# Latent attention of a two-layer block: the 1/rms of the latents applied when queries, keys and values are evicted, and the rotary keys computed in the gate columns' job

## What is computed

```
def rms_norm(x, g):
    y = x * rsqrt(mean(x * x, axis=-1) + EPS)
    return y * g

q_lat, kv_lat, k_rope = split(z, (256, 128, 32))          # z = h @ w_in, per token
q  = (rms_norm(q_lat, g_q_lat) @ w_uq)                    # 4 heads x (64 + 32)
kv = (rms_norm(kv_lat, g_kv_lat) @ w_ukv)                 # 4 heads x (64 keys + 64 values)
q_rope = apply_rope(q[..., 64:96], rot)                   # grid tokens only
k_rope = apply_rope(k_rope, rot)                          # grid tokens only, one for all heads
k = concatenate([k_nope, broadcast(k_rope to 4 heads)])   # 64 + 32
y = softmax(q k^T * 96**-0.5) v
```

## Time and profile before

| what | us |
|---|---|
| median of 3 executions | 4300.83 |
| lowest and highest | 4300.26, 4307.57 |
| the profiled execution, its own time | 4302.52 |
| its span, first to last instruction | 4300.8 |
| layer 0, from the first latent product to the first turn of queries | 57.86 to 174.48 |
| layer 1, the same | 2406.18 to 2509.91 |

### The profile page before, as it was taken

The page is one execution under the profiler, slowest core; times in us unless marked ns, Lnnn a source line. Parts: engine busy times, 40 slices in busy tenths (PEclk is TensorE's granted clock), DMA queues, the critical chain, the costliest instruction groups (busy, mean ns, idle before and its releaser), DMA issues.

```text
span 4300.8 us, 62883 instructions
## 1 busy us (share of the span) xinstructions
PE 3689.4 (86%) x25844; PEld 2503.2 (58%) x25844; DVE 1177.2 (27%) x2860; ACT 769.2 (18%) x1604; POOL 127.7 (3%) x184
## 2 busy tenths in 40 slices
PE   7699999997999599999997669998978957777785
PEld 4355675665776377777775445666657734444443
DVE  0333342425642411111111152325246131111111
ACT  2221322012212200000001321312122120100101
POOL 0000000000000000000000000000000000000000
PEclk9799999998999699999999679898968979999998
DMA  4172111010011199999998101110100239999998
GB/s 185 69 275 97 42 45 44 11 69 1 25 69 69 67 341 343 328 346 351 344 342 321 44 0 37 50 49 30 69 1 30 103 108 383 378 379 381 382 373 304
DMA packets 326559, 740.25 MB, mean 172 GB/s; under 512 B 7808, under 2 KB 79488, under 8 KB 326288
## 3 DMA queue, kind: packets, MB, share of 16 engines
q1 hardware_dynamic: 314800, 695.29, 44.4%
q0 software_dynamic: 11616, 43.05, 3.5%
HBM read 713.09 MB, written 25.21 MB: 172 GB/s over the span
## 4 chain that ended last, share of the span: by engine, by line
PE 66%; DMA 16%; DVE 10%; ACT 5%; issue 3%; DVEq 0%; ACTq 0%; SPq 0%; POOL 0%; POOLq 0%
PE bank L544 11%; PE bank L962 9%; PE bank L472 7%; PE bank L935 7%; PE bank L465 5%; DMA ring<-in_w_e_up 5%; PE bank L926 4%; DMA ring<-in_w_e_gate 4%; PE bank L835 3%; DMA f_rows<-work,idx 3%; PE bank L634 3%; ACT work L1039 3%; DMA ring<-in_w_e_down 3%; PE bank L546 2%; DVE work L1487 2%
## 5 line engine op out<-in xcount | busy, mean ns | idle before, releaser
L544 PE MATMUL bank<-HT,ring 128*128 128x256 f32 x2560 | 637.9, 406 | 15.9 <-DVEq L1552 7.8
L544 PEld LDWEIGHTS bank<-HT,ring 128*128 128x128 f32 x2560 | 517.9, 205 | 122.6 <-issue 25.3
L962 PE MATMUL bank<-ring,work 128*96 128x512 f32 (+1 forms) x1408 | 472.7, 604 | 30.1 <-DMA ring<-in_w_e_down 28.2
L926 PE MATMUL bank<-ring,work 128*64 128x256 f32 x1536 | 384.1, 408 | 130.8 <-DMA ring<-in_w_e_up 71.9
L935 PEld LDWEIGHTS bank<-work,ring 128*64 128x64 f32 x11264 | 475.7, 139 | 16.8 <-issue 15.0
L935 PE MATMUL bank<-work,ring 128*64 128x96 f32 x11264 | 481.9, 249 | 4.2 <-DVEq L2023 3.0
L926 PEld LDWEIGHTS bank<-ring,work 128*64 128x64 f32 x1536 | 218.2, 147 | 271.1 <-DMA ring<-in_w_e_up 90.1
L927 PE MATMUL bank<-ring,work 128*64 128x256 f32 (+1 forms) x1536 | 369.2, 379 | 0.0
L962 PEld LDWEIGHTS bank<-ring,work 128*96 128x96 f32 (+1 forms) x1408 | 167.8, 152 | 298.7 <-issue 265.9
L1039 ACT ACTIVATE work<-bank,small 128x512 f32<-128x512 f32 (+3 forms) x248 | 144.6, 583 | 958.7 <-PE bank L962 500.5
L472 PE MATMUL bank<-ring,HT 128*128 128x512 f32 (+2 forms) x960 | 310.8, 488 | 0.5 <-DVEq L1552 0.5
(11 more groups left out here) (180 smaller groups left out, 3408.4 us busy)
## 6 DMA issues: line engine op xcount, KB each, us to landing
ring<-in_w_e_gate SPq DMA_DIRECT2D x64, 2048.0 KB, 10.4
ring<-in_w_e_up SPq DMA_DIRECT2D x64, 2048.0 KB, 13.5
ring<-in_w_e_down SPq DMA_DIRECT2D x64, 2048.0 KB, 9.6
ring<-in_w_ada SPq DMA_DIRECT2D x24, 2048.0 KB, 8.8
ring<-in_w_e_gate SPq DMA_DIRECT2D x32, 1536.0 KB
ring<-in_w_e_up SPq DMA_DIRECT2D x32, 1536.0 KB, 7.1
ring<-in_w_e_down SPq DMA_DIRECT2D x32, 1536.0 KB, 9.9
ring<-in_w_gate SPq DMA_DIRECT2D x16, 2048.0 KB, 8.6
```

Of the source, the lines that this page charges most:

```text
L544: pe.matmul(b[:, 0:256], w[:, k, d4 * P:(d4 + 1) * P], HT[:, k, off:off + 256], start=(k == 0), stop=(k == KD - 1))
L926: pe.matmul(b[0:64, 0:256], e_xs[:, k, 0:64], w[:, k, 0:256], start=(k == 0), stop=(k == KD - 1))
L962: ins = pe.matmul(banks[6 + half][lo:lo + cap, :], e_hidT[:, at, 0:cap], w[:, k, half * 512:half * 512 + 512], start=(f == 0), stop=(f == ...
```

## The change

- The three blocks of latents are evicted by ACT twice: once squared into `a_sq`, once times the gain `g` into `a_ql` or `a_kv`, without the 1/rms. DVE no longer squares or scales.
- The sums of squares are made with the squares stationary and one column of ones moving, so that each token's sum stands on its own partition, one column for each tile (`squares_of`). Those of the queries stand ahead of the gate columns' job, those of the kv latent behind it. ACT's root and DVE's reciprocal are now on at most 6 columns.
- The six `tm` jobs of the rotary keys are gone. The gate columns' job takes 72 columns instead of 40, with the rotary keys on partitions 0 to 31 of the bank; six transposes turn them to tokens on partitions.
- The queries move from ring "a" and ACT to ring "d" and DVE, which scales a tile by its 1/rms as it evicts it and rotates it at once. The grid's tiles come first.
- Keys and values are scaled by 1/rms as ACT evicts them; ACT waits for the reciprocal (`mla_n`) once, ahead of them.
- The four rotary key tiles are rotated together, in six instructions, and copied to the four heads in one.
- TensorE waits for `mla_kv` (ACT) and `mla_rope` (DVE) before it turns queries and keys.

```diff
-                for t in range(NT):
-                    tm(w, 384, 32, t)
+                def squares_of(rows, tiles):
+                    b = job("a")
+                    for t in tiles:
+                        for i in rows:
+                            ins = pe.matmul(b[:, t:t + 1], a_sq[:, i, t * P:(t + 1) * P], ones[:, 0:1],
+                                            start=(i == rows[0]), stop=(i == rows[-1]))
+                    ins.then_inc(sems["a_done"], 1)
+
+                pe.wait_ge(sems["mla_q"], c.nth("mla_q"))
+                squares_of((0, 1), QT)
                 for off, n in SEG:
-                    fm(w, 416, 40, off, n)
+                    fm(w, 384, 72, off, n)
                 used(n0)
-                pe.wait_ge(sems["mla_sq"], c.nth("mla_sq"))
...
-                pe.wait_ge(sems["mla_n"], c.nth("mla_n"))
+                pe.wait_ge(sems["mla_c"], c.nth("mla_c"))
+                squares_of((2,), range(NT))
                 uq = pk("w_uq").rearrange("p (i n) -> p i n", i=2)
-                for t in QT:
-                    b = job("a")
+
+                def queries(t):
+                    b = job("d")
                     for i in range(2):
                         ins = pe.matmul(b[:, 0:384], a_ql[:, i, t * P:(t + 1) * P], uq[:, i, :], start=(i == 0), stop=(i == 1))
-                    ins.then_inc(sems["a_done"], 1)
+                    ins.then_inc(sems["d_done"], 1)
+
+                first = [t for t in QT if t >= CT]
+                queries(first[0])
+                pe.wait_ge(sems["mla_kr"], c.nth("mla_kr"))
+                b = job("d")
+                for t in range(NT):
+                    ins = pe.transpose(b[:, t * 32:(t + 1) * 32], a_krf[0:32, t * P:(t + 1) * P], ident[0:32, 0:32])
+                ins.then_inc(sems["d_done"], 1)
+                for t in first[1:] + [t for t in QT if t < CT]:
+                    queries(t)
                 for t in range(NT):
                     b = job("a")
                     pe.matmul(b[:, :], a_kv[:, t * P:(t + 1) * P], pk("w_ukv"), start=True, stop=True).then_inc(sems["a_done"], 1)
+                pe.wait_ge(sems["mla_kv"], c.nth("mla_kv"))
                 pe.wait_ge(sems["mla_rope"], c.nth("mla_rope"))
```

ACT's part:

```diff
+                def latents(dst, sq, gain, off, n):
+                    act.wait_ge(sems["a_done"], c.nth("a_done"))
+                    b = bank()
+                    do(sq[:, off:off + n], b[:, 0:n], AF.Square)
+                    do(dst[:, off:off + n], b[:, 0:n], AF.Identity, scale=gain)
+                    act.sem_inc(sems["a_free"], 1)
+
+                def roots(i, tiles, width):
+                    act.wait_ge(sems["a_done"], c.nth("a_done"))
+                    b = bank()
+                    do(s_lat[:, i, tiles[0]:tiles[-1] + 1], b[:, tiles[0]:tiles[-1] + 1], AF.Sqrt, scale=1.0 / width, bias=cc("eps"))
+                    act.sem_inc(sems["a_free"], 1)
+                    act.sem_inc(sems["mla_r"], 1)
+
...
+                roots(0, QT, 256)
                 for off, n in SEG:
                     act.wait_ge(sems["a_done"], c.nth("a_done"))
                     b = bank()
-                    copy(a_kv[:, off:off + n], b[:, 0:n])
+                    copy(a_krf[0:32, off:off + n], b[0:32, 0:n])
+                    copy(gI[0:8, off:off + n], b[32:40, 0:n])
+                    copy(gF[0:8, off:off + n], b[64:72, 0:n])
                     act.sem_inc(sems["a_free"], 1)
...
+                act.sem_inc(sems["mla_kr"], 1)
+                roots(1, range(NT), 128)
+                act.wait_ge(sems["mla_n"], c.nth("mla_n"))
                 for t in range(NT):
                     act.wait_ge(sems["a_done"], c.nth("a_done"))
                     b = bank()[:, :].rearrange("p (h c) -> p h c", h=4)
-                    copy(a_ktm[:, t, :, 0:64], b[:, :, 0:64])
-                    copy(a_v[:, t, :, :], b[:, :, 64:128])
+                    do(a_ktm[:, t, :, 0:64], b[:, :, 0:64], AF.Copy, scale=s_lat[:, 1, t:t + 1])
+                    do(a_v[:, t, :, :], b[:, :, 64:128], AF.Copy, scale=s_lat[:, 1, t:t + 1])
```

DVE's part:

```diff
-                S(dve.reciprocal(a_r[:, 0, q0:T], a_r[:, 0, q0:T]))
-                S(dve.reciprocal(a_r[:, 1, :], a_r[:, 1, :]))
...
+                S(dve.reciprocal(s_lat[:, 0, QT[0]:NT], s_lat[:, 0, QT[0]:NT]))
+
+                def queries(t):
+                    dve.wait_ge(sems["d_done"], c.nth("d_done"))
+                    b = bank()
+                    ts(a_qtm[:, t, :, :], b[:, 0:384].rearrange("p (h c) -> p h c", h=4), s_lat[:, 0, t:t + 1], ALU.mult)
+                    dve.sem_inc(sems["d_free"], 1)
+                    if t >= CT:
+                        rope(a_qtm[:, t, :, 64:96], t, 4, a_tmp)
+
+                first = [t for t in QT if t >= CT]
+                dve.wait_ge(sems["mla_r"], c.nth("mla_r"))
+                S(dve.reciprocal(s_lat[:, 1, :], s_lat[:, 1, :]))
                 dve.sem_inc(sems["mla_n"], 1)
-                dve.wait_ge(sems["mla_tm"], c.nth("mla_tm"))
-                for t in range(CT, NT):
-                    rope(a_qtm[:, t, :, 64:96], t, 4, a_tmp)
-                    rope(a_kr[:, t, :], t, 1, a_tmp)
-                for t in range(NT):
-                    copy(a_ktm[:, t, :, 64:96], a_kr[:, t, :].unsqueeze(1).to_broadcast([P, 4, 32]))
+                queries(first[0])
+                dve.wait_ge(sems["d_done"], c.nth("d_done"))
+                b = bank()
+                copy(a_kr, b[:, 0:NT * 32].rearrange("p (t c) -> p t c", t=NT))
+                dve.sem_inc(sems["d_free"], 1)
+                rope(a_kr[:, CT:NT, :], None, NT - CT, a_tmp)
+                copy(a_ktm[:, :, :, 64:96], a_kr.unsqueeze(2).to_broadcast([P, NT, 4, 32]))
+                for t in first[1:] + [t for t in QT if t < CT]:
+                    queries(t)
                 dve.sem_inc(sems["mla_rope"], 1)
```

More of the change, by code:

```diff
@@ L413, in hybrid_layers @@
         s_soft = small[:, 412:424].rearrange("p (i t) -> p i t", i=2)
+        s_lat = small[:, 412:424].rearrange("p (i t) -> p i t", i=2)
         s_top = small[:, 424:488].rearrange("p (i c) -> p i c", i=8)
@@ L569, in mla @@
+                pe.wait_ge(sems["mla_q"], c.nth("mla_q"))
+                squares_of((0, 1), QT)
                 for off, n in SEG:
-                    fm(w, 416, 40, off, n)
+                    fm(w, 384, 72, off, n)
                 used(n0)
-                pe.wait_ge(sems["mla_sq"], c.nth("mla_sq"))
-                for off, n in QS:
-                    b = job("a")
-                    pe.matmul(b[:, 0:n], ones, a_sq[:, 0, off:off + n], start=True, stop=False)
-                    pe.matmul(b[:, 0:n], ones, a_sq[:, 1, off:off + n], start=False, stop=True).then_inc(sems["a_done"], 1)
@@ L577, in mla @@
-                for off, n in SEG:
-                    b = job("a")
-                    pe.matmul(b[:, 0:n], ones, a_sq[:, 2, off:off + n], start=True, stop=True).then_inc(sems["a_done"], 1)
-                pe.wait_ge(sems["mla_n"], c.nth("mla_n"))
+                pe.wait_ge(sems["mla_c"], c.nth("mla_c"))
+                squares_of((2,), range(NT))
                 uq = pk("w_uq").rearrange("p (i n) -> p i n", i=2)
-                for t in QT:
-                    b = job("a")
+                def queries(t):
+                    b = job("d")
@@ L1117, in mla @@
             def mla(L):
+                def latents(dst, sq, gain, off, n):
[10 more added lines that the diff above has]
+                    act.sem_inc(sems["mla_r"], 1)
                 for i in range(2):
                     for off, n in QS:
-                        act.wait_ge(sems["a_done"], c.nth("a_done"))
-                        b = bank()
-                        copy(a_ql[:, i, off:off + n], b[:, 0:n])
-                        act.sem_inc(sems["a_free"], 1)
+                        latents(a_ql[:, i, :], a_sq[:, i, :], pk("g_q")[:, i:i + 1], off, n)
+                act.sem_inc(sems["mla_q"], 1)
+                for off, n in SEG:
+                    latents(a_kv, a_sq[:, 2, :], pk("g_kv"), off, n)
+                act.sem_inc(sems["mla_c"], 1)
+                roots(0, QT, 256)
                 for off, n in SEG:
@@ L1572, in tab @@
                 def tab(name):
+                    if t is None:
+                        return cc(name).rearrange("p (t a f) -> p t a f", t=groups, a=2)
                     v = cc(name)[:, (t - CT) * 16:(t - CT + 1) * 16].rearrange("p (a f) -> p a f", a=2)
```

41 lines of the change are left out of this document (3 added, 38 removed).

## The result

| what | before, us | changed, us |
|---|---|---|
| median | 4304.14 (4 executions) | 4208.83 (4 executions) |
| lowest and highest | 4300.26, 4307.57 | 4205.88, 4213.57 |
| the profiled execution | 4302.52 | 4206.81 |
| its span | 4300.8 | 4205.1 |
| mean granted clock | 0.909 | 0.917 |

The ratio is 0.978, with a 95% interval of 0.9763 to 0.9797: 95 us faster. In two later comparisons, on two chips, the ratios were 0.9797 [0.9775, 0.982] and 0.9809 [0.9793, 0.9826]. So 84 to 95 us, by medians.

A forecast was written before the change was run, and what follows sets the result against it. The changed stage was taken as a serial chain, one engine after another. Gains 16.1 + 17.1 + 34.6 + 33.4 + 2 = 103.2 us took the profiled 4302.5 to 4199.3, the median to 4198 us, range 4186 to 4214.

The forecast's parts named there:

- its own unknowns: Whole kernel: narrow product price, spread copy, ACT's scale, warm start and small handovers give 4189 to 4207 us, chance 0.72.
- Ahead of G: Latent stage up to the gate job's end: narrow key jobs go, gate job quickens, sums added; gains 16.1 and 17.1 us.
- G: The moment the gate columns' job ends and the next weights are asked for: 119.85 us in layer 0, 2461.30 in layer 1.
- Behind G: Gate job's end to first turn of queries: 54.6 and 48.6 us become 20.0 and 15.2, gaining 34.6 and 33.4.
- The spread copy: DVE's one copy of 768 rotary key elements to the four heads, before the grid tiles, taken as 1.0 us.
- What starts behind: Turns and first scores: part of their half clock start may go, 1 us a layer, 2 us in all.
- Everything behind is shifted, not changed: Attention, other mixers and experts after the stage: keep their lengths, their weight requests shifting along; no gain or loss counted.
- fall in the new narrow work: Rival: clock falls in the sums and behind the gate job, costing 13 us, about 4211 us; chance 0.14.
- Late weights: Rival: first attention starts 35 us sooner after the request, one fetch about 8 us late, 4206 us; chance 0.05.
- 72 columns cost more than 40: Gate job: more stationary columns would cost more, one way of having no measurable gain; chance 0.01.
- The slower case: Rival: TensorE stays at half clock through the first attention, up to 150 us more, about 4347 us; chance 0.02.
- Its counterargument: Against half clock through the first attention: every row shows the clock returning within six us of work.

The follow-up runs named there:

- mixing them: Key and value jobs placed between the remaining query tiles on TensorE instead of behind them, against the changed kernel: median 4214.44 us.
- the comparison on one chip: Before and changed kernels, each plain and with layer 1's first attention 512 column score product made twice: means 4308.0 and 4221.2 us plain, 4301.5 and 4205.5 twice.
- the third trace of the changed kernel: The changed kernel run once more without any edit: median 4221.50 us, four executions.

## Why the prediction held, and which step was off

The forecast was 4198 us in a range of 4186 to 4214; the median was 4208.83. That lies in the range, but above the 4189 to 4207 that its own unknowns gave. Of the 11 us between, 3.3 are the base, since a fourth execution moved the median before from 4300.83 to 4304.14 us, and the rest is a gain that fell short: against the profiled execution the sum was 103.2 us and 95.7 were found. The mechanism of the stage was right; that the median fell inside the range has some luck in it, since the two later medians of the same kernel, 4214.38 and 4221.50 us, lie above it.

- *Ahead of G.* Expected 16.1 and 17.1 us, found 62.0 - 46.3 = 15.7 and 55.1 - 39.2 = 15.9 (from the first latent product to G). The narrow products cost 0.107 each (2.57 us for 24), just below the lower bound of 0.111. (Of my two rows for them, the products of 2 columns don't have the full stationary tile that I wrote: 64 partitions, not 128.) The gate job took 10.38 us against 10.3. What was short by a us was the latents themselves: 33.31 instead of 32.71 us in layer 0 and 27.11 instead of 25.83 in layer 1, since the clock rose one to three us later from its rest.
- *Behind G.* Expected 20.0 and 15.2 us to the first turn, found 19.9 and 14.8. The prices from the nearest rows held: an eviction with a scale 0.62 us plus its gap (0.65), a rotation 1.55 with gaps, ACT's twelve evictions 6.47 us (6.5). The spread copy was priced too dear, 1.0 us where it took 0.56, near its lower bound of 0.48. In layer 0 the bank of the third grid tile and the keys and values behind it ended the stage, as worked out; mixing them gained 3.7 us there, as expected, which the times of the whole didn't show.
- *What starts behind.* Two us expected, 0.6 + 0.8 found up to the first score. The transposes did run at 1.00 (124.10 to 134.40 us), so the rule in the Trainium skill, "TensorE: Matmul & The Clock Gate", Part 4: PE-mode transpose, that the full clock doesn't engage for them, isn't borne out here either.
- *"Everything behind is shifted, not changed".* This is the step that failed. It is right for the weights: TensorE waits for no transfer in layer 0's first attention, before or changed. It is wrong for the clock. I took the granted clock of an attention from 24 us of layer 0's, where it is 1.00, and let it stand for the whole of both. In the trace that I had, layer 0's has one fall in it, and layer 1's, which has no wide adaLN products between its own, works at a mean of 0.84, alternating. Such a stretch doesn't keep its length, not even from one execution of the same kernel to the next. In the first pair layer 1's attention took back 3.7 us and layer 0's 2.6; in the comparison on one chip, about nine us went with layer 1's.
- *The rivals.* The clock did not fall in the new narrow work in the trace of the result; in one of three traces of the changed kernel it did, in layer 0, and the gate job took 1.5 us more. The price of 13 us was too high by far: nothing behind G slowed there, and it took four times the sums to lose 22.6 us. Late weights and "72 columns cost more than 40" are out: the gate job's pace is that of the jobs of 128 columns, 10.3 us. The slower case, half clock through the first attention, has the right mechanism and puts it mainly in the wrong layer, and is worth up to 13 us (87.2 against 74.5), not 150. Its counterargument, that the clock returns within six us of work, fails in layer 1: in the third trace of the changed kernel it stays at 0.50 from 2435 to 2461 us, with TensorE busy 25.67 of those 26.00 us.

## What to carry to other kernels

Factors that belong to a token can wait until an eviction that happens anyway, if the sum that makes them is laid out with tokens on partitions: the wide reciprocals, scalings and their handovers fell from the path, and the price of each scaled eviction could be read from the nearest shapes to within a tenth of a us. A serial stage in which engines wait for each other can be summed piece by piece; but look behind it for stretches with a mean clock between the two levels, because their length isn't fixed: here the same 304 matmuls took 73.6 to 87.2 us. Where such a stretch waits anyway, its waits are the place for other wide products: in the changed kernel even ones that were thrown away gained time.

## What the runs showed of the hardware that I had not expected

- Busy isn't enough for the full clock: in the run with four times the sums TensorE was busy 3.00 of every 3.00 us with products one column wide, and the clock was 0.50; in layer 1's first attention of the changed kernel's third trace it was busy 25.67 of 26.00 us, with products of 64 to 512 columns, and the clock was 0.50 too.
- Work that is thrown away can make a stretch shorter: with 16 products more, layer 1's attention took 76.3 us at 0.98, against 78.2 to 87.2 at 0.77 to 0.64 in the three traces of the same kernel without them.
- The same program's layer 1 attention took from 74.5 to 80.8 us in three traces of the kernel before, and 78.2 to 87.2 in three of the changed one. Single executions of before ranged from 4292.9 to 4319.5 us.
- Narrow work didn't always take as long to bring the clock down: it fell 2.2 to 5.0 us after the first narrow product, in four traces.
